# Mixing stage of a hybrid two-layer kernel: exponents of the third recurrence in blocks of four levels

## What is computed

```python
def hgrn2_run(args, s0, with_out):
    q, lg, kk, v = args
    ...
    G = jnp.cumsum(lg, axis=2)
    ...
    dec = jnp.exp(jnp.where(mask[:, :, None, None], G[:, :, :, None] - G[:, :, None, :], -jnp.inf))
    Aw = jnp.einsum('bcihk,bcjhk,bcijhk->bcijh', q, kk, dec)
    o = jnp.einsum('bcijh,bcjhv->bcihv', Aw, v) + jnp.einsum('bcihk,bchkv->bcihv', q * jnp.exp(G), starts)
```

## Time and profile before

| | us |
|---|---|
| median of 3 runs | 5588.89 (5584.56 to 5596.67) |
| profiled execution, its own time | 5593.15 |
| its span, first to last instruction | 5591.3 |
| PE busy | 5134.1 (92%) |
| DVE, ACT, POOL busy | 2815.2, 1830.4, 2478.7 |
| mixing, first layer | from 1258 to about 1832 |
| mixing, second layer | from 4048 to about 4560 |

### The profile page before, as it was taken

One profiled execution on the slowest core, in us unless ns is written; L12 is line 12 of the kernel. 1 busy time (PEld: TensorE's weight loads), 2 busy tenths in 40 slices (PEclk: granted clock), 3 DMA queues, 4 the chain that ended last, 5 costly groups with the idle time before them and its releaser, 6 DMA issues. The chain is left out here.

```text
span 5591.3 us, 68589 instructions
## 1 busy us (share of the span) xinstructions
PE 5134.1 (92%) x25238; PEld 2711.6 (48%) x25272; DVE 2815.2 (50%) x4638; ACT 1830.4 (33%) x4021; POOL 2478.7 (44%) x1686
## 2 busy tenths in 40 slices
PE   6999999888888899998989999998688879999989
PEld 2454544456777433332444545444577753333334
DVE  2444534336777555551435346363467765555324
ACT  2222222223434244444012223232234333444422
POOL 1112232314444299998211322323244436899941
PEclk8999999969999799999999999999599988999999
DMA  5444533473221100000433444444632220000032
GB/s 190 135 146 139 168 125 130 145 247 131 99 85 65 54 1 9 8 7 32 177 121 124 154 142 140 142 134 135 198 126 99 89 73 1 8 1 9 5 121 106
DMA packets 411807, 561.53 MB, mean 100 GB/s; under 512 B 103096, under 2 KB 283632, under 8 KB 407120
## 3 DMA queue, kind: packets, MB, share of 16 engines
q1 hardware_dynamic: 391746, 516.72, 27.7%
q10 hardware_dynamic: 19728, 40.41, 1.9%
HBM read 402.67 MB, written 154.06 MB: 100 GB/s over the span
## 5 line engine op out<-in xcount | busy, mean ns | idle before, releaser
L2467 POOL TENSOR_TENSOR attention_PS<-attention_PS 128x1024 f32<-128x1024 f32 x548 | 1265.9, 2358 | 80.3 <-ACT attention_PS L2600 72.9
L2513 DVE TENSOR_REDUCE attention_mxp<-psum 128x1 f32<-128x512 f32 (+1 forms) x1016 | 654.2, 685 | 541.2 <-PE psum L2650 541.2
L2600 ACT ACTIVATE attention_PS<-psum 128x512 f32<-128x512 f32 (+1 forms) x1168 | 630.6, 592 | 717.1 <-PE psum L2704 695.1
L2650 PE MATMUL psum<-attention_QK 32*128 32x512 f32 (+1 forms) x2592 | 772.4, 613 | 9.1 <-DVE attention_mxp L2502 6.1
L657 POOL TENSOR_TENSOR projection_cx<-projection_cx,projection_cw 128x1152 f32<-128x1152 f32 x72 | 196.7, 2733 | 1175.2 <-DMA projection_cx<-xbc 529.7
L2698 PE MATMUL psum<-attention_QK 32*128 32x512 f32 x2336 | 664.4, 642 | 0.0
L2716 PE MATMUL psum<-attention_PS,attention_va 128*64 128x512 f32 x2336 | 627.7, 616 | 0.0
L680 PE MATMUL psum<-group_B,projection_hT 128*128 128x512 f32 (+1 forms) x1360 | 567.0, 561 | 36.1 <-ACT projection_p L819 20.0
L680 PE MATMUL psum<-group_B,projection_S 128*128 128x512 f32 (+1 forms) x1360 | 556.3, 552 | 2.3 <-DVE projection_u L994 2.3
L680 PE MATMUL psum<-projection_T,projection_S 128*128 128x512 f32 (+1 forms) x1360 | 556.1, 551 | 0.0
L680 PEld LDWEIGHTS psum<-group_B,projection_hT 128*128 128x128 f32 x1360 | 261.9, 194 | 303.1 <-issue 263.1
(11 more groups left out here) (395 smaller groups left out, 7529.7 us busy)
## 6 DMA issues: line engine op xcount, KB each, us to landing
group_B<-in_w_in SPq DMA_DIRECT2D x120, 512.0 KB, 7.6
group_B<-in_w_in SPq DMA_DIRECT2D x48, 1024.0 KB, 8.9
projection_cx<-xbc SPq DMA_DIRECT2D x216, 192.0 KB, 3.4
u<-projection_u SPq DMA_DIRECT2D x158, 256.0 KB
mixing_hg<-u SPq DMA_DIRECT2D x34, 1024.0 KB, 5.0
u<-projection_u SPq DMA_DIRECT2D x52, 512.0 KB
output_y<-y SPq DMA_DIRECT2D x34, 512.0 KB, 4.1
xc<-projection_cx SPq DMA_DIRECT2D x72, 192.0 KB, 1.9
```

Of the source, the lines that this page charges most:

```text
L2467: G.tensor_tensor(SA[x % 2][:, rs, 0:w], one[:, rs, 0:w], PT[i % PTB][:, rs, 0:w], ALU.add) \
L2513: bk.release(V.tensor_reduce(mxp[x % 2][:, q:q + nn, 2 * pr + j, a], bk[job, j][:, 0:nn * (hi - lo)].rearrange("p (q n) -> p q n", q=nn), ...
L2600: bk.release(A(PT[i % PTB][:, r, 0:w], bk["st", i, r][:, 0:w], ACT.Exp, scale=scale), ("st", i, r))
L2650: return T(out[:, at:at + hi - lo], QK[rows(r), a0, t * P:(t + 1) * P], QK[rows(r), 2 + a0, lo:hi], start=True, stop=True)
```

## The change

The exponents are no longer made level by level, but in blocks of four levels. For each tile there are again eight jobs, j = 0 to 7, now with one matmul of 512 columns each: j // 4 tells which four levels (0 to 3, or 4 to 7), and the other two bits tell direction d and channel half p. The log decays of (d, p), 128x128, are the weights, and `mats` is laid out so that the four matrices of a direction stand side by side, the one for v = 0 first. The Exp of a job still has 512 elements, and writes them as four runs of 128 into `E0[t % 2]` (levels 0 to 3) or `E1` (levels 4 to 7). A level is complete when the last two of its four jobs are drained (`levels_made`). So jobs run five ahead (`AHEAD`): jobs 0 to 3 of a tile are made at v = 3 to 6 of the tile before, job 4 at v = 7, and jobs 5 to 7 at v = 0 to 2. Five jobs stand before the loop instead of two.

`xk` and `xq` wait for the jobs of their block instead of their own level's; where the wait for a level had kept them behind the matmuls that read the buffer before, they now wait for those matmuls (`("A", t - 1, 7)` at v = 1, `("A", t - 1, 6)` at v = 2). The table loads are four instead of two.

```diff
-    uses = [(("hgT", 0), 4), (("E", 0, 0), 0), (("E", 0, 1), 1)]
+    AHEAD = 5
+    uses = [(("hgT", 0), 4)] + [(("E", 0, j), j % 2) for j in range(AHEAD)]
...
-            if v + 2 < STEPS:
-                uses.append((("E", t, v + 2), v % 2))
-            elif t + 1 < count:
-                uses.append((("E", t + 1, v + 2 - STEPS), v % 2))
+            n, j = divmod(STEPS * t + v + AHEAD, STEPS)
+            if n < count:
+                uses.append((("E", n, j), j % 2))
...
-        E = two("E", [P, 2, 2, P])
-        Ec = two("Ec", [P, 2, 2, P])
+        E0 = two("E0", [P, 4, 2, 2, P])
+        E1 = k.sb(c, "E1", [P, 4, 2, 2, P])
...
-        tri = k.sb(c, "tri", [P, 4, P])
-        mats = k.sb(c, "mats", [P, 2 * LEVELS, P])
+        tri = k.sb(c, "tri", [P, P])
+        mats = k.sb(c, "mats", [P, 2, STEPS, P])
...
-        tables = [(tri[:], k.x["c_tri"]), (mats[:], k.x["c_mats"])]
+        tables = [(mats[:, :, 0], k.x["c_tri"][:, 0:2]), (tri[:], k.x["c_tri"][:, 2])]
+        tables += [(mats[:, d, 1:STEPS], k.x["c_mats"].rearrange("p (v d) n -> p d v n", d=2)[:, d]) for d in range(2)]
...
+        level = lambda t, v: E0[t % 2][:, v] if v < 4 else E1[:, v - 4]
+
+        def levels_made(eng, t, v):
+
+            for j in (2, 3):
+                bk.freed(eng, ("E", t, v // 4 * 4 + j))
...
                     if v >= 3:
                         bk.wait(gp, ("A", t, v - 2))
-                    bk.freed(gp, ("E", t, v))
+                    elif t:
+                        bk.wait(gp, ("A", t - 1, STEPS - v))
+                    levels_made(gp, t, v)
...
-                    if n > 2:
-                        act.wait_ge(s["Xq_ready"], n - 2)
-                        act.wait_ge(s["Xk_ready"], n - 2)
-                    drain(("E", t, v), f3(E[v % 2][:]), ACT.Exp)
+                def exps(t, j):
+                    d, p = j % 4 // 2, j % 2
+                    if j == 0 and t >= 2:
+                        act.wait_ge(s["Xc_ready"], t - 1)
+                        bk.freed(act, ("incmh", t - 2))
+                        act.wait_ge(s["Xq_ready"], LEVELS * (t - 2) + 3)
+                        act.wait_ge(s["Xk_ready"], LEVELS * (t - 2) + 3)
+                    if j == 4 and t:
+                        act.wait_ge(s["Xq_ready"], LEVELS * t)
+                        act.wait_ge(s["Xk_ready"], LEVELS * t)
+                    job = ("E", t, j)
+                    bk.wait(act, job)
+                    out = E0[t % 2] if j < 4 else E1
+                    bk.release(A(out[:, :, d, p], bk[job].rearrange("p (v n) -> p v n", v=4), ACT.Exp), job)
...
                 def xq(t, v):
+                    if v == 1:
+                        bk.freed(dve, ("hgT", t))
                     if v >= 3:
                         bk.wait(dve, ("A", t, v - 2))
-                    bk.freed(dve, ("E", t, v))
+                    elif t:
+                        bk.wait(dve, ("A", t - 1, STEPS - v))
+                    levels_made(dve, t, v)
...
                     bk.take(pe, job)
-                    for d in range(2):
-                        m = mats[:, 2 * (v - 1) + d] if v else tri[:, d]
-                        for p in range(2):
-                            i = 2 * d + p
-                            ins = T(bk[job][:, i * P:(i + 1) * P], hcol(t, "hg_f", i * P, P), m, start=True, stop=True)
-                    bk.done(ins, job)
+                    bk.done(T(bk[job][:], hcol(t, "hg_f", (2 * d + p) * P, P),
+                              mats[:, d, j // 4 * 4:j // 4 * 4 + 4].rearrange("p v n -> p (v n)"), start=True, stop=True), job)
```

More of the change, by code:

```diff
@@ L1789, in xk @@
                         bk.wait(gp, ("A", t, v - 2))
-                    bk.freed(gp, ("E", t, v))
+                    elif t:
+                        bk.wait(gp, ("A", t - 1, STEPS - v))
+                    levels_made(gp, t, v)
                     w = 1 << (v - 1)
                     G.tensor_tensor(skew(Xk[v % 2][:], 0, [[w, 2], [2 * w, P // w], [1, w]]),
-                                    skew(E[v % 2][:], 0, [[256 + w, 2], [2 * w, P // w], [1, w]]),
+                                    skew(level(t, v), 0, [[256 + w, 2], [2 * w, P // w], [1, w]]),
                                     skew(hkT[t % 2][:], 0, [[256 + w, 2], [2 * w, P // w], [1, w]]), ALU.mult) \
@@ L1907, in _ @@
                 turned(0)
-                exps(0, 0)
-                exps(0, 1)
+                for j in range(AHEAD):
+                    exps(0, j)
                 for t in TILES:
                     for v in range(STEPS):
-                        if v + 2 < STEPS:
-                            exps(t, v + 2)
-                        elif t + 1 < count:
-                            exps(t + 1, v + 2 - STEPS)
+                        n, j = divmod(STEPS * t + v + AHEAD, STEPS)
+                        if n < count:
+                            exps(n, j)
                         if v == 6 and t + 1 < count:
@@ L1999, in _ @@
                             hg_loaded(dve, t)
-                            bk.freed(dve, ("E", t, 0))
+                            levels_made(dve, t, 0)
                             bk.freed(dve, ("hgT", t))
-                            V.tensor_tensor(Xc[t % 2][:], Ec[t % 2][:], hqT[t % 2][:].unsqueeze(1).to_broadcast([P, 2, 2, P]),
+                            V.tensor_tensor(Xc[t % 2][:], level(t, 0), hqT[t % 2][:].unsqueeze(1).to_broadcast([P, 2, 2, P]),
                                             ALU.mult).then_inc(s["Xc_ready"], 1)
@@ L2044, in _ @@
                                 sl = slice(ST_HG + p * 64, ST_HG + p * 64 + 64)
-                                ins = V.scalar_tensor_tensor(new[:, sl], old[:, sl], Ec[t % 2][:, 0, p, P - 1:P], m[:, sl],
+                                ins = V.scalar_tensor_tensor(new[:, sl], old[:, sl], level(t, 0)[:, 0, p, P - 1:P], m[:, sl],
                                                              ALU.mult, ALU.add)
@@ L2124, in hg_turn, with exponents @@
                     bk.done(ins, ("hgT", t))
-                def exponents(t, v):
-                    job = ("E", t, v)
-                    if v == 0:
+                def exponents(t, j):
+                    job, d, p = ("E", t, j), j % 4 // 2, j % 2
+                    if j == 0:
                         hg_loaded(pe, t)
                     bk.take(pe, job)
-                    for d in range(2):
-                        m = mats[:, 2 * (v - 1) + d] if v else tri[:, d]
-                        for p in range(2):
-                            i = 2 * d + p
-                            ins = T(bk[job][:, i * P:(i + 1) * P], hcol(t, "hg_f", i * P, P), m, start=True, stop=True)
-                    bk.done(ins, job)
+                    bk.done(T(bk[job][:], hcol(t, "hg_f", (2 * d + p) * P, P),
+                              mats[:, d, j // 4 * 4:j // 4 * 4 + 4].rearrange("p v n -> p (v n)"), start=True, stop=True), job)
                 def weights(t, v):
@@ L2179, in _ @@
                 pe.wait_ge(s["tables_in"], 16 * len(tables))
-                exponents(0, 0)
-                exponents(0, 1)
+                for j in range(AHEAD):
+                    exponents(0, j)
                 pe.wait_ge(s["consts_in"], 16 * len(consts))
@@ L2192, in _ @@
                         weights(t, v)
-                        if v + 2 < STEPS:
-                            exponents(t, v + 2)
-                        elif t + 1 < count:
-                            exponents(t + 1, v + 2 - STEPS)
+                        n, j = divmod(STEPS * t + v + AHEAD, STEPS)
+                        if n < count:
+                            exponents(n, j)
                         if v == 0:
@@ L2211, in _ @@
                             bk.take(pe, ("sum", t))
-                            ins = T(bk["sum", t][:, 0:256], tri[:, 2], hcol(t, "hg_f"), start=True, stop=True)
+                            ins = T(bk["sum", t][:, 0:256], tri[:], hcol(t, "hg_f"), start=True, stop=True)
                             bk.done(ins, ("sum", t))
```

10 lines of the change are left out of this document (1 added, 9 removed).

## The result

The changed kernel takes 5599.7 us in the median (5586.8 to 5608.2) where the kernel before takes 5589.1 beside it: 1.0016 times as long, with an interval of 1.0010 to 1.0023. It is slower by 0.16%, some 9 to 11 us, where 5 us less were forecast. The profiled execution took 5608.17 us (span 5606.3), the highest of its runs, so its counts of unlucky tiles may be higher than those of the median run.

What follows compares the result with a forecast made beforehand. Bound: a path changing engines in each 30.75 us mixing tile, neither PE nor VectorE filling it. Sum: -5.4 (tiles) - 2.4 (start) + 3 (half clock) = -4.8, from 5593.15 to 5588.4, median 5584; range 5569 to 5605.

Steps and rivals of the forecast that it cites:

- The path: Mixing tile: an engine-changing path sets its end; exponents of v = 2 and 6 count, those of v = 3, 4, 5, 7 don't.
- PE's job: Exponents on PE: two 512-column instructions take 0.96 us instead of 1.00, a saving of 0.03 a job.
- the extra 0.10: First weight load of the exponent job on PE, after a 64-row group, is not hidden: 0.10 us more.
- The steady gain: Each mixing tile gets 0.16 to 0.17 us shorter, 5.4 us over 32 tiles' worth.
- ScalarE's start: E of v = 2 waits for one semaphore, not three, and starts 0.04 us earlier; bounds 0 and 0.12.
- The tie: `xk` of v = 1 on GpSimd meets VectorE's last gated-sum operation; first starter locks out the other; VectorE forecast to win.
- rival 1: GpSimd wins that meeting: VectorE's operation ends 0.57 us later, net +0.43 a tile, total 5603, slower; chance 0.25.
- VectorE's lead of 0.02 to 0.07: VectorE's last gated-sum operation was to start 0.02 to 0.07 us before GpSimd's `xk` of v = 1.
- Half clock: Tiles of another length and last tiles without exponents at v = 3 to 5 may add one dip a layer: +3 us.
- Start: Stage start: up to 2.3 us saved by full clock, less 1 for table loads; net -1.2 a layer, -2.4 in all.
- rival 3: PE's clock drops more often, or the four-run write costs its bound: 5588 to 5606, say 5595; chance 0.13.

Runs made afterwards that it cites:

- the tie and the last tile taken away: Changed kernel with GpSimd's `xk` of levels 1 and 2 waiting for `keep`, plus surplus matmul jobs in each layer's last tile: 5581.4 us, ratio 0.9987.
- the kernel with the filled last tile: Changed kernel with four surplus matmul jobs and their Exp, results unread, in the last tile of each layer: 5590.7 us, ratio 1.0003.
- the kernel before with the two holds: Kernel before, with GpSimd's `ksT` waiting for the gated sum and `xk` of level 7 for the subtracted mean: 5586.9 us, ratio 0.9987.
- the kernel with narrow matmuls: Changed kernel with each 512-column job made as four matmuls of 128 columns, all else kept: 5619.7 us, ratio 1.0053.
- that with the tie always lost: Changed kernel with a small VectorE copy ahead of L2106, meant to let GpSimd's `xk` of level 1 start first: 5620.4 us, ratio 1.0048.

## Why the prediction was wrong, point by point

- **The path** held. PE's job, against 0.97: forecast 0.96. L2099 ends 0.28 after `ksT` (1519.45 + 0.64 against 1519.09 + 0.72), as said. PE's waits before `incss` and `own` are those of the earlier trace rows less 0.1; forecast 1.45, measured 1.45. The first of the job's two instructions takes 0.53 to the start of the second, the second 0.43 to the next group, as in a stream; the extra 0.10 stands where the prediction had put it:

```profile
1501.18 0.59 PE L2147 MATMUL psum<-mixing_mats,mixing_hg 128*128 128x512 f32 x1
```

The Trainium skill's gap for an isolated matmul (TensorE: Matmul & The Clock Gate, Back-to-back issue gap) is 0.216 us for 512 columns. Counted twice for each of the two fp32 instructions, as one takes 0.429 in a stream, it gives an estimate of 0.86 for the job; the trace has 0.97. The same page (LDWEIGHTS (loading the stationary operand)) gives P / 1.2 ns for a weight load of P columns; for 128 that is an estimate of 0.11 us, and the trace's extra 0.10 agrees with it.
- **The steady gain** was put at 0.16 to 0.17 us a tile and is 0.20 by the means, 0.19 by the medians of undisturbed tiles. The width gives 0.12, exactly 4 x 0.03. The term that was too small seems to be ScalarE's start, 0.04 (no run changes it alone): E follows the exponents' end by 0.04 now (1500.64 + 1.13 to 1501.81 in its timeline), not by 0.08, where the earlier trace rows had 0.12.
- **The tie** is the step that failed. Its place and the rule were right, and its price nearly: +0.67 on the tile, where rival 1 gave 0.57. Two things were wrong. `ysum` was to come 0.05 to 0.1 later against `ksT`; it comes 0.04 later (1519.45 - 1519.09 = 0.36 against 1520.11 - 1519.79 = 0.32 in the earlier trace rows). So L2106 starts not 0.02 to 0.07 but 0.09 to 0.10 after the end of `weights(t, 7)`, and `xk` starts 0.09 after it, as forecast: VectorE's lead of 0.02 to 0.07 is 0.00. And I took the tie for one decision for all tiles, so that forecast and rival excluded each other. With a lead of nothing, nanoseconds decide tile by tile; a third of the tiles was lost, and that cost 7 us, between my 0 and the 18 of all tiles lost (32 x 0.57).
- **Half clock** was mis-sized, +3 for +7.4. The text names the last tile without exponents at v = 3 to 5, but prices it as a dip of 1.4 us like that of the earlier trace rows. What came is the last 15 of 34 us of that tile at 1.2 GHz on PE's path, 3.5 us in each layer. That PE's waits grow by 0.03 to 0.06 only holds for a tile in the middle, not for the last.
- **Start**: -2.4 was forecast, about nothing came. The tables arrive 1.5 and 1.1 us later after the start of the stage (first exponents after 9.95 and 9.64 us, 8.49 and 8.52 before), near the 1 that I took. But the full clock that was to bring up to 2.3 came only in part: the idle time before the loop is 3 us now, and in the 4.6 us after it the granted clock is 0.63 in both layers, where the kernel before had 0.50 and 0.65. The first L2106 comes 46.1 and 45.4 after the start without its lost tie, against 46.25 and 45.6. PE in the changed kernel, and the stretch after the start of its loop:

```profile
1266.30 6.45 PE L2147 MATMUL psum<-mixing_mats,mixing_hg 128*128 128x512 f32 x10 [2.33 <-DMA mixing_mats<-in_c_mats]
1275.79 0.71 PE L2160 MATMUL psum<-mixing_hqT,mixing_ksT 64*128 64x128 f32 x8 [3.04 <-POOL mixing_ksT L1811]
```

```profile
1275.79:1280.39 4.60, 4.60 (x24) 3.10 (x26) 2.07 (x3) 1.63 (x3) 3.30 (x4) 0.63 0.93 313
```

PE starts the loop 19.45 after the start of the stage, where 18.28 had passed before.
- **The chances.** Rivals 1 and 3 came true in part and together: a third of the ties, and half clock in the last tiles more than in further dips. The range of rival 3 holds 5599.7, but without a tie. That these two turned a gain into +10.6 is shown by the runs: with the tie and the last tile taken away, 20 us are back, and the kernel is ahead of the one before.

## What to carry to other kernels

When an edit moves the start of a GpSimd operation, look for the VectorE operation that it lands on, and give GpSimd a wait that decides the order; a lead of some ten nanoseconds is no lead, and here a tie cost a third of the tiles the whole operation. When an edit takes matmul work out of a stage that is limited by waits, ask where PE's idle time piles up, at the end of a loop above all: at half clock the rest of the tile is dearer than the work that was saved, and surplus matmuls in a wait can be cheaper than none.

## What was new of the hardware

- Two instructions that start within some nanoseconds are still ordered strictly. In the changed kernel VectorE ran with GpSimd up to 4 ns ahead and waited from 7 ns on, and then for all of GpSimd's operation; in the kernel with the filled last tile a lead of 5 ns went one way in one tile and the other way in another. The Trainium skill (SBUF — State Buffer, SBUF: two separate sides) says that whoever starts first holds the pair for the whole instruction; every tile of the changed kernel agrees: L2106 takes 0.42 to 0.43 us, or, where `xk` is 7 to 21 ns ahead, 1.09 to 1.11 (0.99 at the first tile of each layer, where `xk` is 0.14 us ahead).
- PE's waits, none of them longer than 1.7 us within a layer, are enough for half clock. Tiles with a clock of 0.89 to 0.95, in the profiled executions: two in the kernel before at 30.72 us a tile, four in the changed kernel at 30.52 and ten with its last tile filled, seven at 30.49 and at 30.35, nine in the kernel before with the two holds at 30.33, nine and sixteen at 30.15, five in the kernel with narrow matmuls and seven in that with the tie always lost (besides its one at 0.77); none once two surplus matmuls stood in PE's waits, at 30.49, 30.30 and 30.15 alike. Each cost at most 1.5 us. What sets their number is not settled: the length of the tile doesn't by itself, as four and ten at 30.52 and nine and sixteen at 30.15 show.
- A copy with a single input in SBUF waits for GpSimd's operation like one with two (0.85 us for 0.17, above).
